# Row norms between the first weight slots, weight splits inside the attention sequences, and a new order of loads, in a two-layer decoder trunk

## The reference, cut to what matters

```python
def rms_norm(x, g):
    y = xf * lax.rsqrt(jnp.mean(xf * xf, axis=-1, keepdims=True) + RMS_EPS)
    return (y * g.astype(jnp.float32)).astype(x.dtype)
...
    h = x
    mem_n = rms_norm(mem, mem_norm_g)
    for layer in range(DEPTH):
        xn = rms_norm(h, norm_g[layer])
        mem_kv = mem_n @ mem_w_kv[layer]
        ...
        h = h + (mixed @ w_out[layer]).astype(h.dtype)
    return rms_norm(h, final_norm_g)
```

## Time and profile before

| | us |
|---|---|
| median of 3 runs | 2443.32 (2438.5 to 2444.15) |
| profiled execution, its own time | 2440.99 |
| its span | 2439.4 |
| PE busy | 2320.8 |
| DVE busy | 994.4 |
| ACT busy | 813.4 |
| POOL busy | 374.1 |

### The profile page before, as it was taken

One profiled execution on the slowest core, in us unless ns is written; L12 is line 12 of the kernel. 1 busy time (PEld: TensorE's weight loads), 2 busy tenths in 40 slices (PEclk: granted clock), 3 DMA queues, 4 the chain that ended last, 5 costly groups with the idle time before them and its releaser, 6 DMA issues.

```text
span 2439.4 us, 30550 instructions
## 1 busy us (share of the span) xinstructions
PE 2320.8 (95%) x11816; PEld 1880.5 (77%) x11816; DVE 994.4 (41%) x1827; ACT 813.4 (33%) x1453; POOL 374.1 (15%) x633
## 2 busy tenths in 40 slices
PE   5999999999999989999899999999999989999995
PEld 5888888888888768878677778788887756777784
DVE  4632355444422255642343332442122256666423
ACT  5432333333323333422232222222222444444321
POOL 7404112111110001100010001000000243221100
PEclk9999999999999999999999999999999999999998
DMA  9644434443335245553343446344534644544531
GB/s 250 194 128 136 131 105 118 118 122 114 110 110 186 82 150 183 171 209 100 116 125 118 131 143 222 104 134 135 159 98 128 210 151 148 177 150 134 201 95 69
DMA packets 165081, 345.58 MB, mean 142 GB/s; under 512 B 20775, under 2 KB 31303, under 8 KB 162003
## 3 DMA queue, kind: packets, MB, share of 16 engines
q1 hardware_dynamic: 106368, 186.41, 25.6%
q0 software_dynamic: 30464, 102.61, 13.2%
q10 hardware_dynamic: 28115, 54.73, 6.2%
HBM read 279.88 MB, written 63.82 MB: 141 GB/s over the span
## 4 chain that ended last, share of the span: by engine, by line
PE 90%; DVE 3%; issue 2%; DMA 2%; POOL 1%; ACT 1%; DVEq 0%; POOLq 0%; ACTq 0%
PE PS L212 75%; PE PS L1513 3%; PE PS L1502 1%; PE PS L2149 1%; PE PS L2012 1%; DMA hA<-stage 1%; PE PS L957 1%; PE PS L953 1%; PE PS L1683 1%; PE PS L1825 1%; PE PS L930 1%; PE PS L1708 1%; PE PS L903 1%; DMA S<-in_x_dram 1%; PE PS L2037 1%
## 5 line engine op out<-in xcount | busy, mean ns | idle before, releaser
L212 PE MATMUL PS<-A,wsp 128*128 128x512 f32 (+1 forms) x5232 | 1179.1, 385 | 18.1 <-DVE wsp L185 9.1
L212 PEld LDWEIGHTS PS<-A,wsp 128*128 128x128 f32 x5232 | 949.5, 188 | 218.2 <-issue 21.8
L185 DVE TENSOR_TENSOR wsp<-wraw,wsp 128x1024 fp32r<-128x1024 f32 (+2 forms) x366 | 432.3, 1187 | 1138.7 <-ACT wsp L181 1138.2
L212 PE MATMUL PS<-wsp,A 128*128 128x512 f32 x3072 | 788.6, 402 | 19.3 <-DVE wsp L185 6.3
L181 ACT ACTIVATE wsp<-wraw 128x1024 fp32r<-128x1024 f32 (+2 forms) x366 | 372.4, 1024 | 1039.3 <-PE PS L212 1002.9
L212 PEld LDWEIGHTS PS<-wsp,A 128*128 128x128 f32 x3072 | 561.2, 190 | 127.2 <-issue 17.7
L272 ACT ACTIVATE stage<-PS 128x512 f32<-128x512 f32 (+1 forms) x150 | 85.9, 587 | 128.5 <-PE PS L212 122.9
L1549 ACT ACTIVATE S<-PS 128x256 f32<-128x256 f32 (+3 forms) x160 | 63.1, 394 | 159.3 <-PE PS L1502 136.4
L1513 PEld LDWEIGHTS PS<-S 128*128 128x128 f32 x640 | 93.6, 192 | 13.3 <-issue 3.2
L1513 PE MATMUL PS<-S 128*128 128x128 f32 x640 | 95.4, 276 | 2.8 <-issue 2.6
L1557 ACT ACTIVATE S<-PS,stats 128x256 f32<-128x256 f32 (+3 forms) x160 | 74.7, 467 | 62.0 <-DVE stats L1593 54.0
(11 more groups left out here) (310 smaller groups left out, 1733.0 us busy)
## 6 DMA issues: line engine op xcount, KB each, us to landing
wraw<-in_even_w_in_dram SPq DMA_DIRECT2D x112, 512.0 KB, 3.7
wraw<-in_odd_w_in_dram SPq DMA_DIRECT2D x88, 512.0 KB, 3.6
wraw<-in_w_out_dram SPq DMA_DIRECT2D x80, 512.0 KB, 3.8
wraw<-in_mem_w_kv_dram SPq DMA_DIRECT2D x32, 512.0 KB, 4.5
yO<-stage ACTq DMA_DIRECT2D x12, 1024.0 KB
yE<-stage ACTq DMA_DIRECT2D x10, 1024.0 KB
S<-yO POOLq DMA_DIRECT2D x36, 256.0 KB, 3.4
hA<-stage ACTq DMA_DIRECT2D x8, 1024.0 KB
```

The source lines that it names most:

```text
L185: nc.vector.tensor_tensor(wsp[:, q, 1, :, 0:j["cols"]], wraw[:, q, :, 0:j["cols"]], wsp[:, q, 0, :, 0:j["cols"]].bitcast(F32), ALU.subtrac ...
L212: mm = nc.tensor.matmul(dst, lhs, rhs, start=(s == 0 and kk == 0 and i == 0), stop=(s == j["spc"] - 1 and kk == 1 and i == 2))
```

## The change

- In a chunk's last slot the matmuls run bank by bank, so the banks end one after the other, and readers of GLU, OUT0B and OUT1B wait for each bank (`bank_done`).
- `NORMS[0]` and `NORMS[2]`: ScalarE runs a Sqrt on a spare column ahead of the squares. Row tiles are scaled in two pieces (512 and 1536 columns), half of them on ScalarE (`act_scale`). Four column tiles come before the first slot, the other twelve in pairs behind the slots (`pe_norm`). Each memory tile has its own semaphore. Three splits of O1 are made before the last adds of layer 0.
- `NORMS[1]`: squares, factor and the first eight tiles come later in the memory jobs. POOL issues its loads of x only after both squares of the memory rows.
- Between E2 and GLU: the low parts of z (`dve_z`) are made in pairs from E2's slots on, the product z times gate (`dve_zg`) moves from E2 into E1's last chunk, in halves.
- OUT0A starts with no bank wait. In both sequences 48 fill matmuls run in step 0; OUT0B's and OUT1B's first four splits are made inside the sequence; the residual adds are spread over steps, store and load come later; chunks of SEQ1 end one step sooner. OUT0B and OUT1B wait for heads pair by pair (`pe_chunk_of_heads`); OUT1A starts before the last latent head is finished.
- `pool_mla` replaces `pool_att`: q, k and v of a head are loaded before its rotary part is turned, and the gate of the odd head before both.
- The final norm: three of four column chunks are multiplied by the gain inside OUT1B (`dve_gain`), the factor is applied by VectorE and ScalarE, and SP stores the output, not POOL.

```diff
+                if s == j["spc"] - 1:
+                    kk, f = m // 3 % 2, m // 6
...
+                if j is OUT0A and c == 0:
+                    pass
+                elif kk == 0 and s == 0 and i == 0 and free[f] is not None:
                     pe.wait_ge(banks_free, free[f])
...
-                if j["stage"] and s == j["spc"] - 1 and kk == 1 and i == 2 and f < nf - 1:
+                if s == j["spc"] - 1 and kk == 1 and i == 2 and f < nf - 1:
...
-            if isinstance(c, int) and c == 0:
+            if j in (OUT0B, OUT1B) and c == 0:
+                free = [j["bank0"] - 3 + f for f in range(4)]
+            elif isinstance(c, int) and c == 0:
...
-            act.wait_ge(*((mem_in, 32) if v["k"] == 0 else (rows_in[t], 16)))
+            act.wait_ge(*((mem_in[t], 16) if v["k"] == 0 else (rows_in[t], 16)))
...
+        PIECES = (slice(0, 512), slice(512, D))
+
+        def act_scale(act, v, i, piece):
+            act.wait_ge(rows_ok, ROWS0[v["k"]] + 1)
+            cs = PIECES[piece]
+            nc.scalar.activation((scaled if v["k"] == 2 else hrows)[:, i, cs], hrows[:, i, cs], ACT.Copy, scale=small[:, 20 + i:21 + i]).then_inc(rows_act, 1)
+
+        def act_sqrt_ahead(act):
+            act.wait_ge(ident_ok, 4)
+            nc.scalar.activation(spare[:, 0:1], one_sb[:, 0:1], ACT.Sqrt)
...
             if k == 0:
-                pe.wait_ge(rows_ok, [0, 3, 8][v["k"]] + 1 + v["tiles"])
+                pe.wait_ge(rows_ok, ROWS0[v["k"]] + 1 + [1, 4, 2][v["k"]])
+            if k == 4 and v["k"] != 1:
+                pe.wait_ge(rows_ok, ROWS0[v["k"]] + 1 + [2, None, 4][v["k"]])
+            if k in (0, 4) and v["k"] != 1:
+                pe.wait_ge(rows_act, {(0, 0): 1, (0, 4): 2, (2, 0): 4, (2, 4): 6}[v["k"], k])
...
-        def pe_norm(pe, v):
-            for k in range(KD):
+        def pe_norm(pe, v, j):
+
+            def following(s):
+                for k in (2 * s + 4, 2 * s + 5):
+                    if k < KD:
+                        pe_tile(pe, v, k)
+                if s < 7:
+                    pe.wait_ge(nt_lo, KD * v["k"] + 2 * s + 4)
+            for k in range(4):
                 pe_tile(pe, v, k)
-
-
+            pe.wait_ge(nt_lo, KD * v["k"] + 2)
+            pe_chunk(pe, j, 0, following)
...
-            if (job_, s) in ((0, 2), (0, 4), (0, 6), (1, 0)):
-                act_square(act, NORMS[1], ((0, 2), (0, 4), (0, 6), (1, 0)).index((job_, s)))
-            if (job_, s) == (1, 2):
+            if job_ == 1 and 3 <= s < 7:
+                act_square(act, NORMS[1], s - 3)
+            if (job_, s) == (1, 7):
...
+        def dve_z(dve, i):
+
+            dve.wait_ge(slot_used, GLU["slot0"] - E2["spc"] + 5 + i)
+            for k in (2 * i, 2 * i + 1):
...
+        def dve_zg(dve, h):
+            dve.wait_ge(gelu_ok, 3 + h)
+            part = slice(2048 * h, 2048 * h + 2048)
+            nc.vector.tensor_tensor(S[:, 4096:8192][:, part], S[:, 0:4096][:, part], S[:, 4096:8192][:, part], ALU.mult).then_inc(zg_ok, 1)
...
-            act.wait_ge(slot_used, GLU["slot0"] + 4 * (c + 1))
             for f in range(4):
                 k = 4 * c + f
+                act.wait_ge(*((bank_done, GLU["done0"] + 3 * c + f + 1) if f < 3 else (slot_used, GLU["slot0"] + 4 * (c + 1))))
...
-                dve.wait_ge(slot_used, j["slot0"] + j["spc"] * (c + 1))
+                dve.wait_ge(*((bank_done, j["done0"] + 3 * c + t + 1) if t < 3 else (slot_used, j["slot0"] + j["spc"] * (c + 1))))
...
-            def odd_gate(b):
-
-                wait(pool, t.fin0, b, 2, -2)
-                pool.dma_start(t.inp[1][-1], yO[ds(num(b, 2, -1 - 2 * t.b0) * P + 4096, P), :]).then_inc(t.gl[1], 16)
...
-                gate = load(pool, num(b, 2, h - 2 * t.b0), h % 2, t.ld[h % 2])
...
+        def pool_mla(pool, t):
+
+            def gate(r, head, row):
+                wait(pool, t.fin0, *head)
+                pool.dma_start(t.inp[r][-1], yO[ds(num(*row) * P + 4096, P), :]).then_inc(t.gl[r], 16)
+
+            gate(0, (t.b0, 2, -1), (t.b0, 2, -2 * t.b0))
+            pool_sum(pool, qrS, 1)
             with pool.Fori(t.b0 + 1, t.b0 + t.pairs) as b:
-                for h in range(2):
-                    one(b, h)
-            if t is MLA:
-                odd_gate(t.b0 + t.pairs)
+                h = num(b, 2, -2 * t.b0)
+                pool_rotary_load(pool, h)
+                gate(1, (b, 2, -2), (b, 2, -1 - 2 * t.b0))
+                wait(pool, t.sc, b, t.upp, -t.uph)
+                wait(pool, t.vtp, b, 2, t.v0 - 1)
+                mla_qkv(pool, h, 0, t.ld[0])
+                pool_rotary_turn(pool, h)
+                pool_sum(pool, qrS, 0)
+                wait(pool, t.sc, b, t.upp, 0)
+                wait(pool, t.vtp, b, 2, t.v0)
+                mla_qkv(pool, num(b, 2, 1 - 2 * t.b0), 1, t.ld[1])
+                pool_sum(pool, qrS, 1)
+                gate(0, (b, 2, -1), (b, 2, -2 * t.b0))
+            gate(1, (t.b0 + t.pairs, 2, -2), (t.b0 + t.pairs, 2, -1 - 2 * t.b0))
...
+                    if c == 0:
+                        want = max(want, 48)
...
+                self.first_splits = {1: () if l else (2, 3), 2: tuple(n for n in range(4, N_FILL + 4) if self.pe_end[n - 4] < 2)}
+                self.splits = {x: tuple(n for n in range(4, N_FILL + 4) if self.pe_end[n - 4] + 1 == x) for x in range(3, self.steps + 1)}
+                assert sum(map(len, self.splits.values())) + len(self.first_splits[2]) == N_FILL
...
+                if c == 0 and t.l == 1 and m0 % 24 == 0:
+                    pe.wait_ge(MLA.fin, MLA.done - 6 + 2 * s)
...
+        def pe_chunk_of_heads(pe, j, fin0):
+
+            pe.wait_ge(a_fin, fin0 + 2)
+            pe_chunk(pe, j, 0, lambda s: pe.wait_ge(a_fin, fin0 + 2 * s + 4) if s < 5 else None)
...
-                if x == e + 2:
+                if x == e + 3 + 2 * t.l:
                     act_store(act, j, c)
-                if x == e + 4 and c < 3:
+                if x == e + 6 + 5 * t.l and c < 3:
...
-                    if x == e + 1:
-                        seq_add(dve, t, c)
-                seq_split(dve, lambda e, n, q, r: dve_slot(e, j, n, q), t, [n for n in range(4, N_FILL) if t.pe_end[n - 4] + 1 == x])
+                    for f in range(4):
+                        if x == e + 1 + (f // 2 * (1 + t.l) + f % 2 * t.l if c < 3 else 0):
+                            seq_add(dve, t, c, f)
...
-            pool.wait_ge(nt_pe, 3 * KD)
+            pool.wait_ge(rows_ok, ROWS0[2] + 5)
+            pool.wait_ge(rows_act, 6)
...
-        SEQ1 = Seq(1, [u for h in range(8) for u in nsa_head(h)] + [u for h in range(4) for u in mem_head(1, h, yO, 3584, 6144, 320, 192)], OUT1A, h1D, 2)
+        SEQ1 = Seq(1, [u for h in range(8) for u in nsa_head(h)] + [u for h in range(4) for u in mem_head(1, h, yO, 3584, 6144, 320, 192)], OUT1A, h1D, 3)
...
+        def dve_gain(dve, c):
+            if c == 0:
+                dve.wait_ge(gf_in, 16)
+            for t in range(4):
+                dve.wait_ge(sq_done, NORMS[3]["sq0"] + 4 * c + t + 1)
+                part = hrows[:, t, c * COLS:(c + 1) * COLS]
+                nc.vector.tensor_tensor(part, part, gfS[:, c * COLS:(c + 1) * COLS], ALU.mult).then_inc(hg_ok, 1)
+
         def dve_final(dve):
-            dve_norm(dve, NORMS[3])
+            dve_var(dve, NORMS[3])
+            dve_rms(dve, NORMS[3])
+            dve.wait_ge(hg_ok, 12)
             r = small[:, 20:24]
-            dve.wait_ge(rows_ok, 14)
-            dve.wait_ge(gf_in, 16)
+            last = slice(3 * COLS, 4 * COLS)
             for t in range(4):
-                nc.vector.scalar_tensor_tensor(hrows[:, t, :], hrows[:, t, :], r[:, t:t + 1], gfS, ALU.mult, ALU.mult).then_inc(fin_ok, 1)
+                if t < 2:
+                    nc.vector.tensor_scalar(hrows[:, t, 0:3 * COLS], hrows[:, t, 0:3 * COLS], r[:, t:t + 1], None, ALU.mult).then_inc(fin_ok, 1)
+                nc.vector.scalar_tensor_tensor(hrows[:, t, last], hrows[:, t, last], r[:, t:t + 1], gfS[:, last], ALU.mult, ALU.mult).then_inc(fin_ok, 1)
+
+        def sp_out(sp):
+            for t in range(TT):
+                sp.wait_ge(fin_ok, (2, 4, 5, 6)[t])
+                if t >= 2:
+                    sp.wait_ge(fin_act, t - 1)
+                sp.dma_start(out[t * P:(t + 1) * P, :], hrows[:, t, :]).then_inc(out_sem, 16)
+            sp.wait_ge(out_sem, 64)
...
+            pool.wait_ge(sq_done, 2)
...
-            act_norm(act, NORMS[0])
-            pend = lambda: None
-            for n_, j in enumerate(plan[:4]):
+            act_sqrt_ahead(act)
+            act_square(act, NORMS[0], 0)
+            act_square(act, NORMS[0], 1)
+            act_root(act, NORMS[0])
+            act_split(act, plan[0], 0)
+            act_scale(act, NORMS[0], 1, 0)
+            act_tiles(act, NORMS[0], (0, 1))
+            act_split(act, plan[0], 1)
+            act_scale(act, NORMS[0], 1, 1)
+            act_tiles(act, NORMS[0], (2, 3))
+            for s in range(2, 8):
```

(40 more changed lines are left out.)

204 lines of the change are left out of this document (98 added, 106 removed).

## The result

The changed kernel takes 2381.32 us, the median of 4 runs (2379.44 to 2382.5), against 2442.86 (2438.5 to 2444.15) for the kernel before in 4 runs: ratio 0.975, 95% interval 0.9739 to 0.9761, so 61.5 us or 2.5% less. Predicted were 2383 and a range of 2366 to 2404. The profiled execution took 2381.5 us, its span 2379.9; the mean granted clock is 0.992 (0.985 before).

A forecast was written before the change was run, and what follows sets the result against it. The tensor engine was taken as the bound, busy 2320.8 of 2439.4 us and standing in few places. Eight terms, 11 + 6.5 + 6 + 6 + 9.5 + 8.7 + 9 + 3.3 = 60.0 us, gave 2383 us, 80% range 2366 to 2404.

The forecast's parts named there:

- signs of being wrong: Engine standing between slots in first 70 us, idle in steps 1 to 12, or low clock as often as before.
- rivals 1 to 3: Start stays with the DMA; nothing won in the sequences; waits return under other names; chances 0.12, 0.13, 0.10.
- A: Start, memory norm: first weight matmul at about 17.0 us, part given back to tiles and late weights; 11 us gained.
- Rival 1: Start stays bound by the DMA; A falls to 2, time 2392 us; chance 0.12.
- B: Between E2 and GLU: low parts made earlier, wait before GLU shrinks; 5.5 and 1.0 of clock, 6.5 us.
- C: Out of GLU into OUT0A: wait for all eight sigmoids goes, low clock shrinks; 4.9 + 1.1 = 6.0 us.
- D: Into OUT0B and OUT1B: last head's finish and first split hidden; 2 x 2.6 + 0.8 of clock = 6.0 us.
- G: Inside SEQ0 and SEQ1: 10 us of idle taken back, 1.5 lost in steps without fill, SEQ0 gains 0.5; 9.0 us.
- Rival 2: Nothing won in the sequences, steps without fill run at softmax latency; G falls to -4, time 2396 us; chance 0.13.
- E: Norm of layer 1, OUT0B to O1: first slot 17.0 us earlier, less 7.4 for tiles and low clock; 9.5 us.
- F: Latent heads: score 5.2 us earlier, 2.3 of clock, 1.2 at the end; 8.7 us.
- H: Final norm to the end: shorter chain 2.7, first row 0.6, queue's issuing not counted; 3.3 us.

The follow-up runs named there:

- even fill: Changed kernel without the rule that 48 fill matmuls run in step 0, fill spread evenly in both sequences; 2372.6 us.
- the splits moved: Changed kernel with SEQ0's splits of slots 2 and 3 in step 0, both sequences' slots 4 and 5 in steps 5 and 7; 2382.8 us.
- The last version: Changed kernel without 48 fill matmuls in step 0 and, in SEQ0 alone, a chunk's four residual adds in one step; 2375.67 us, ratio 0.9721.
- E0: Not a run but a job of the kernel; its first weight matmul comes 126.6 us after the start in the changed kernel, 134.8 in the kernel before.

## Why the prediction was right, and where its steps failed

The reading held: the tensor engine stood in few places, those were the joins, and the change removed them. That the sum came out within 2 us is partly luck. The terms for the sequences were too high by 13.6 us, those for the norm, the latent heads and the end too low by 13.5 together. Of its own signs of being wrong two came in part: the engine stood between slots at 41.8 and in the first steps of SEQ0, and the second sequence took 227.7 us, not under 222. Two slips don't bear on the sum: 1968.92 + 2 x 1.26 + 1.27 is 1972.7, and the chances of the forecast and rivals 1 to 3 add up to 0.97, not 0.96.

- **A, 11, measured 8.2** (3.8 to 10.1 over the nine traces of the same start). The first matmul at 17.0 was right (17.63). The 1.1 given back to late weights (12.1 taken as 11) were too few: slots 0 to 4 ran without a stop, and slots 5 and 6 and memv0 waited. Rival 1 named the mechanism; its price of 9 was too high.
- **B, 6.5, measured 7.7.** The idle 6.18 is 0.83, which gives the 5.4 up to GLU and is the same in every trace. The low clock behind it, in GLU, cost 2.3 and not 1.0 (46.06 and 43.79 us for the same matmuls).
- **C, 6.0, measured 4.9 in this kernel.** The wait went; its clock did not. The low clock of 910.0 to 916.8 stood behind OUT0A's first matmul (911.76), so in SEQ0, and there the changed kernel has as long a one behind its new stop. With even fill or with the splits moved that one is gone. The cause named, 24 matmuls ahead of the scores, isn't needed: with even fill there is no wait either.
- **D, 6.0, measured 7.9**: twice the wait of 3.15, and 1.6 of the clock behind OUT1B's start.
- **G, 9.0, measured -4.6.** The step that failed: "steps 1 to 5 of SEQ0 and 1 to 12 of SEQ1 have no fill; the softmax chain may show there, 1.5 lost". It lost 7 in SEQ0 (-3.8 less the 3.15 of D), which are 4.9 us of waits and the low clock behind them, and some 2.6 in SEQ1. I had counted VectorE's time as an average over the stretch and hadn't asked what it does in the very steps that were emptied: the splits of slots 2 to 5 were put there by the same change. In SEQ1 the gain beside D is 5.5 - 3.15 = 2.4 and not 8.5; the 10 us "taken back" of 14.2 idle weren't reached, since of 10.4 us of waits for exponentials and transposes 8.2 stay (4.6 and 3.6). Rival 2, G at -4, was right in kind and in size. With either remedy SEQ0 gains 3.6 to 4.1: the 3.15 of D and the 2.5 of the old low clock, less 1.5 of longer waits for `stage`. The last version, without those waits, gains 5.7.
- **E, 9.5, measured 14.4** to O2, 12.9 of it by O1's tenth slot. O1's first slot came 17.0 earlier, as predicted to a tenth, and the twelve tiles cost 5.5 (predicted 5.4). Mis-sized was the clock: 2 us were given back for slot 0, but in this trace the low clock fell on the transposes, and the 1.5 us that O1's first slot had lost to it before (6.89 for 5.44) were gained instead. The 1.5 us of the bank order in O1's last chunks were not in the sum at all.
- **F, 8.7, measured 12.0** to OUT1A's first matmul. The turn's place is worth 7.0 to 9.2 (predicted 5.2 and 2.3 of clock). With the turn put back the stretch is still 2.8 under the kernel before; that this is the end of the last head, taken at 1.2, no run isolates.
- **H, 3.3, measured 8.6.** Of it 4.8 is the queue, which I had set at nothing ("what the other queue saves in issuing, isn't counted"). The earlier trace rows ended at 2434.3 and the span at 2439.4: those 5 us stood in the rows, unasked. The rest, 3.7, is the term.

The clock's share: up to the last matmul the kernel before has nine stretches at the low level, 54.6 us together, the changed kernel six, 23.9 us. If the engine had worked through all of them, 27.3 and 11.9 us would be lost, so at most 15.4 of the 59.5 us are the clock's; the busy time of the same 11816 matmuls fell by 11.7. The low clock went where its stop went, and stayed or came where a stop did.

Open: what else than the clock makes the latent heads scatter by 2.2 us; what one pair of splits costs alone; and what of A could be had by fewer bytes, which wasn't tried.

## What to carry to other kernels

Before work is moved into a stretch "where the engine is half idle", list what that engine does in the very steps it moves to: fill taken out of a step and splits put into it are each free, and together they stopped the tensor engine for 7 us. Judge an in-order queue by its head: a late x held the weight splits for 12 us, a late preparation for 9. And read the end of the profile from the last data to the end of the span, not only to the last instruction. Look at the clock of a stretch before two traces of it are compared.

## What the runs showed of the hardware

- Stores by POOL's queue end the span 5.1 us behind their last data, those by SP's 0.9 us (21.5 against 16.7 us from the last matmul), in two kernels that differ in nothing else.
- With the same code, E0 starts anywhere from 124.7 to 131.0 us after the span's start; 4.6 of these 6.3 us are there at memk1 (73.0 to 77.7). The starts at 129.2 to 131.0 have 10.2 us of low clock ahead of E0, the others 3.4 or 6.8. Behind E0 five stretches repeat within 0.1 us and four scatter by 1.2 to 3.9.
- The same instructions of SEQ1 take 225.1, 227.7 and 229.0 us with 0, 6.8 and 10.2 us at the low clock, at 10 us of idle time each.
- The profile's 1.00 at the very start isn't what the engine did: the first eight transposes take 1.94 us, eight of the same form at 132 us 1.03 (changed kernel), and those under a recorded low clock have the pace of the first (3.32 us for sixteen at 1190.30).

```profile
15.35 1.94 PE L448 MATMUL PS<-ident,S 128*128 128x128 f32 x8 [15.35 <-ACT S L372]
...
132.13 1.03 PE L448 MATMUL PS<-ident,S 128*128 128x128 f32 x8
```

- With S5's parameters among them, the loads of 24 to 36 us keep the DMA engines at a share of 1.05 while only 210 GB/s move (264 of 1149 packets are under 512 B); with the parameters held back, the weights take 0.60 of the engines' time at 191 GB/s (80 of 1190 packets):

```profile
24.00:36.00 12.00, 11.35 (x96) 11.11 (x96) 5.68 (x9) 4.41 (x8) 1.94 (x3) 1.00 1.05 210
```

```profile
24.00:36.00 12.00, 12.00 (x104) 12.00 (x103) 7.93 (x12) 6.18 (x10) 0.00 (x0) 1.00 0.60 191
```

The first row is the changed kernel's, the second that of the one with late parameters.
